# A hybrid attention and pooling block on one core: the query tiles' cosine products on VectorE, and one token sum between the two gate halves

## The reference, cut to what matters

```python
z = rms_norm(h, norm_gain)                       # h: 16 meta tokens + 2048 tokens, 1024 wide
proj = einsum("bld,de->ble", z, w_in)
q, k, v, g_attn, u_pool, g_pool = split(proj)
q = partial_rotary(q); k = partial_rotary(k)     # 16 of each head's 64 features turn
o_attn = chunked_window_attention(q, k, v, attn_sinks)
o_pool = multiscale_pool_mixer(u_pool, w_pool, pool_scale)
gated = concat([silu(g_attn) * o_attn, silu(g_pool) * o_pool])
h = h + einsum("ble,ed->bld", gated, w_out)
y = rms_norm(h, final_norm_gain)[:, 16:]
```

## Time and profile before

| what | value |
|---|---|
| time, median of 3 runs | 1256.24 us (1254.01 to 1257.84) |
| the profiled execution's own time | 1256.06 us |
| its span | 1254.3 us |
| PE busy | 1223.2 us, 98% |
| DVE busy | 804.5 us, 64% |
| ACT busy | 583.7 us, 47% |
| POOL busy | 203.6 us, 16% |
| mean granted TensorE clock | 0.994 of full speed |

### The profile page before, as it was taken

The page is one execution under the profiler, slowest core; times in us unless marked ns, Lnnn a source line. Parts: engine busy times, 40 slices in busy tenths (PEclk is TensorE's granted clock), DMA queues, the critical chain, the costliest instruction groups (busy, mean ns, idle before and its releaser), DMA issues.

```text
span 1254.3 us, 16673 instructions
## 1 busy us (share of the span) xinstructions
PE 1223.2 (98%) x6017; PEld 988.2 (79%) x6017; DVE 804.5 (64%) x1280; ACT 583.7 (47%) x1372; POOL 203.6 (16%) x238
## 2 busy tenths in 40 slices
PE   9999988999999999999999999998999999999997
PEld 9788767877777777788888788886777777788886
DVE  6553332366666666876676977666767666696757
ACT  6622221245555555444755334234555555543445
POOL 1157677520000000500001210000000000100000
PEclk9999999999999999999999999999999999999999
DMA  9525665421110101863254313327111101163324
GB/s 356 203 84 185 224 228 196 161 95 34 34 34 34 37 33 49 320 244 117 86 180 170 119 67 101 134 99 262 34 34 37 47 36 35 53 233 101 113 89 168
DMA packets 46319, 152.57 MB, mean 122 GB/s; under 512 B 4656, under 2 KB 8272, under 8 KB 46256
## 3 DMA queue, kind: packets, MB, share of 16 engines
q1 hardware_dynamic: 29328, 90.45, 21.2%
q0 software_dynamic: 16928, 61.25, 13.4%
HBM read 119.70 MB, written 35.91 MB: 124 GB/s over the span
## 4 chain that ended last, share of the span: by engine, by line
PE 83%; DVE 5%; POOL 5%; issue 3%; ACT 2%; DMA 2%; DVEq 0%; SPq 0%; ACTq 0%; POOLq 0%
PE ps L1423 14%; PE ps L1425 14%; PE ps L1424 14%; PE ps L1713 7%; PE ps L1714 7%; PE ps L1715 7%; PE ps L1614 3%; PE ps L1685 2%; PE ps L1659 2%; PE ps L1598 2%; PE ps L1600 2%; PE ps L1599 2%; POOL tq L587 1%; PE ps L1687 1%; POOL ta_g L577 1%
## 5 line engine op out<-in xcount | busy, mean ns | idle before, releaser
L1423 PE MATMUL ps<-zh,wsplit 128*128 128x512 f32 x912 | 362.1, 397 | 11.1 <-DVE gates_all L1089 8.9
L1425 PE MATMUL ps<-zh,wsplit 128*128 128x512 f32 x912 | 357.3, 392 | 0.0
L1424 PE MATMUL ps<-zl,wsplit 128*128 128x512 f32 x912 | 357.1, 392 | 0.0
L987 DVE TENSOR_TENSOR wsplit<-wraw,wsplit 128x1024 fp32r<-128x1024 f32 (+1 forms) x132 | 174.3, 1321 | 113.1 <-ACT wsplit L657 90.9
L1423 PEld LDWEIGHTS ps<-zh,wsplit 128*128 128x128 f32 x912 | 172.5, 189 | 47.2 <-DVE gates_all L1089 10.6
L1425 PEld LDWEIGHTS ps<-zh,wsplit 128*128 128x128 f32 x912 | 172.2, 189 | 37.1
L1424 PEld LDWEIGHTS ps<-zl,wsplit 128*128 128x128 f32 x912 | 172.6, 189 | 34.3
L1713 PE MATMUL ps<-wsplit,gsh 128*128 128x512 f32 x448 | 174.6, 390 | 1.9 <-DVE gsl L1328 1.7
L1714 PE MATMUL ps<-wsplit,gsh 128*128 128x512 f32 x448 | 174.3, 389 | 0.0
L1715 PE MATMUL ps<-wsplit,gsl 128*128 128x512 f32 x440 | 171.2, 389 | 0.0
L657 ACT ACTIVATE wsplit<-wraw 128x1024 fp32r<-128x1024 f32 x112 | 119.7, 1069 | 93.2 <-PE ps L1715 68.2
(11 more groups left out here) (224 smaller groups left out, 1722.0 us busy)
## 6 DMA issues: line engine op xcount, KB each, us to landing
wraw<-wt SPq DMA_DIRECT2D x32, 512.0 KB, 3.2
wraw<-in_wa SPq DMA_DIRECT2D x26, 512.0 KB, 4.2
wraw<-in_wq SPq DMA_DIRECT2D x24, 512.0 KB, 3.5
wraw<-wat SPq DMA_DIRECT2D x17, 512.0 KB, 3.2
tq<-in_wq POOLq DMA_DIRECT2D x8, 1024.0 KB, 6.4
wt<-tq POOLq DMA_DIRECT2D x8, 1024.0 KB, 5.6
wraw<-wc SPq DMA_DIRECT2D x16, 512.0 KB, 3.3
wraw<-in_wb SPq DMA_DIRECT2D x16, 512.0 KB, 3.5
```

The source lines that it names most:

```text
L987: ve.tensor_tensor(wl[:, slot, 0:size], wraw[:, slot, 0:size], wh[:, slot, 0:size].bitcast(F32), ALU.subtract).then_inc(w_lo, 1)
L1423: te.matmul(ps[:, PB[bank], :], w_h, rhs_z(zh, tb, k), start=k == 0, stop=False)
L1424: te.matmul(ps[:, PB[bank], :], w_h, rhs_z(zl, tb, k), start=False, stop=False)
L1425: last = te.matmul(ps[:, PB[bank], :], w_l, rhs_z(zh, tb, k), start=False, stop=k == KT - 1)
```

## The change

It does three things. `times_cos` of the query tiles goes from POOL to DVE, in both halves: a new `times_cos` in DVE's block is called in `pair_a` behind the second `split_lo` and ahead of `rotate`. The key tile's stays on POOL. Sum 2 of half 1's first pair goes from ahead of `swap` to between the two `silu`, ahead of sum 3. The stream's own two lines for the cosines become a call of the new function, with the same instruction at the same place.

```diff
@@ POOL, in for j in range(HT)
                         gp.dma_start(tq[:, :, :], wq[:, j // 2, :, cols].rearrange("q p n -> p q n")).then_inc(t_in, 16)
-                    if h == 0 or j < PAIR0:
-                        times_cos((1 + HT) * h + 1 + j)
                     pair = PAIR0 + j - 1
@@ DVE, behind swap
+                def times_cos(r):
+
+                    dve.wait_ge(rot_sw, r + 1)
+                    ve.tensor_tensor(rotsrc[:, :], rotsrc[:, :], cos_t[:, :], ALU.mult).then_inc(rot_cos, 1)
+
@@ DVE, pair_a
                     swap((1 + HT) * h + 1 + j)
                     split_lo(block_a(h, 4 + 2 * j), 0)
+                    times_cos((1 + HT) * h + 1 + j)
                     rotate((1 + HT) * h + 1 + j, qk[:, :, 1 + j, :])
@@ DVE, half 1
-                    SUMS = [((0, 1, 2), (3,)), ((4, 5, 6), (7,)), ((8, 9), ())]
+                    SUMS = [((0, 1), (2, 3)), ((4, 5, 6), (7,)), ((8, 9), ())]
@@ DVE, half 1, in the stream
-
                             done = r if prod == 3 else r - 1
-                            dve.wait_ge(rot_sw, done + 1)
-                            ve.tensor_tensor(rotsrc[:, :], rotsrc[:, :], cos_t[:, :], ALU.mult).then_inc(rot_cos, 1)
+                            times_cos(done)
                             rotate(done, qk[:, :, done - (1 + HT) * h, :])
```

## The result

Four runs of the changed kernel took 1240.26 us in the median (1239.6 to 1241.6), four of the kernel before 1255.65 (1254.01 to 1257.84). The ratio is 0.9878, with an interval from 0.9859 to 0.9896: faster by 1.2%, outside what run to run can give. The forecast was 1240.6.

What follows compares the result with a forecast made beforehand. PE, busy 98% of the span, bounds the kernel; stalls and lower clock cost 13.03 us in half 0 and 4.05 in half 1. 17.1 - 1.5 = 15.6 us off 1256.24 gives 1240.6 us; range 1238.0 to 1247.5.

Steps and rivals of the forecast that it cites:

- Part 1: Half 0: with the cosines off POOL, whose round outlasts PE's pair, the 13.03 us of stalls go, save a residue.
- S + 6.95: Half 0's pairs: forecast end of the first SiLU without held instructions, in us from the shuffle's start S.
- The residue: Half 0: cost left from POOL's subtractions holding DVE, 1.5 us in all, between bounds of nothing and 7.5.
- S + 10.2: Half 0's pairs: when PE needs the first SiLU, in us from the shuffle's start; 3.2 us to spare.
- one or two: Half 0: DVE instructions forecast as held by POOL's train of four subtractions at 122 to 128.
- three held instructions, just at the limit: Half 0: three holds of some 1.1 us end the SiLU 10.25 us behind the shuffle's start, just at the limit.
- how often?: Half 0: placing POOL's rounds, every 24.9 us from 93, against DVE's pairs; most pairs stay just inside the limit.
- the lock takes much of it back: Rival, half 0: three pairs stall 1.2 us and lose the clock, 9.3 us, giving 1248.3 us; chance 0.14.
- Part 2: Half 1's first pair: sum 2 behind the first SiLU starts the shuffle earlier; no stall, the full 4.05 us won.
- Part 3: The stream's call: the same instruction at the same place, so nothing gained or lost.
- the rival on DVE's side: Rival, half 0: DVE becomes the bound, slower; seven pairs cost 28 us, giving 1267 us; chance 0.02.
- other releaser: Rival: something besides POOL's cosine product holds the SiLU, PE waits as long, 1254 to 1257 us; chance 0.03.

Runs made afterwards that it cites:

- before_no_subs: The kernel before, with POOL's 52 subtractions on weights replaced by memsets of one element: 1244.95 us, ratio 0.9909.
- one_more: The changed kernel, with one more low-part subtraction on DVE in half 0's pairs, a repeat that changes no value: 1254.73 us, ratio 0.9997.
- sums_only: The kernel before, with only the new place of the token sum; the cosine products stay on POOL: 1251.52 us, ratio 0.9971.
- four_more_no_subs: The changed kernel without POOL's subtractions on weights, with half 0's low part written five times instead of once: 1257.12 us, ratio 1.0023.

## Why the prediction held, and where not

**Part 1, the cause.** Right. POOL's lateness came from its round, and `before_no_subs` shows it: a product on POOL costs half 0 no stall once the round is short. The chain without it came out to the hundredth, S + 6.94 where S + 6.95 was forecast, and that was luck in part. From the cosines' product to the addition were 1.45 us and not 1.36, and the addition took 1.14 to its successor and not its full 1.23; the two errors cancel. POOL's last store moved with it, to 247.93, forecast near 247.

**The residue.** Forecast 1.5 us, measured 0.96, but partly by compensation. The meetings were placed by adding up POOL's rounds. The pair that begins at 126.06 had three held instructions, where "one or two" were forecast. The prediction's own rounds, 93 and then every 24.9 us, put a second train at 131.2, beside that pair's addition, and it was not counted. The last three pairs had none, where "one" was said of one of them. The limit was set at S + 10.2 and was S + 9.82. The step behind it takes PE's readiness (S + 10.2) for the limit; the 0.3 us for filling PE again, which the prediction adds to a stall, belongs off it, and gives S + 9.9. So "three held instructions, just at the limit" is a loss of 0.3 to 0.6 us.

**The size of the cost, in its form.** The prediction treated the hits as independent, 1.1 us each, and the expectation of `one_more` followed that rule: at most 1247.5, where 1254.7 was measured. The term that failed in that expectation is the prediction's "how often?": it took POOL's rounds and PE's pairs as given, one beside the other. A stretched pair changes the next meeting, and behind two of the stalls came the clock. The rival "the lock takes much of it back" lay one DVE instruction a pair away, and would then have cost 14.5 us where it was priced at 9.3.

**Part 2.** Right: by the trace the shuffle followed the second sum, PE had no wait for a SiLU in half 1, and the full 4.05 us came back. `sums_only` shows that this part needs nothing of part 1. The second SiLU, behind two sums, ended in time as well.

**Part 3.** Right: nothing.

**The clock.** That 1.66 us did not lower the clock and 2.15 us did was used as a threshold on length: against the lock's rival, and for the point at S + 12.3 of the rival on DVE's side. The runs do not bear it out. Over all thirteen profiled runs, PE's waits for a SiLU in the pairs and for the last rotated tile before scores lowered the clock in none of 9 of 1.1 to 1.7 us, in 1 of 10 of 1.8 to 2.0, in 6 of 13 of 2.1 to 2.3, and in 10 of 12 of 2.7 to 3.3. Among the same waits some ended either way: 1.84 us in `one_more` and in `four_more_no_subs`, 2.29 and 2.28 us in two profiles of the change itself. So length raises the chance and does not settle it. In the change no such stall was left in the pairs, so the forecast did not suffer; the scores' wait and its clock were there before the change too.

**The other rivals.** No other releaser stood behind L528, and DVE did not become the bound, in a kernel as it is. With four more writes a pair it did, by the chain that was drawn for that rival: 2.15 us a pair at the upper clock.

## What to carry to other kernels

A product on a slow helper engine can be harmless or can cost 12 us, and its duration doesn't tell which: compare the helper's round with the period of the work that waits for it, and look at what is queued ahead. When two engines hold each other up and each runs in a loop, compute their periods; a margin smaller than one or two held instructions can turn into a loss in nearly every iteration, so test it by adding one instruction. And where a sum and a product feed the same wait, do each alone, since their gains don't add.

## What the runs showed of the hardware

- DVE's instructions with two SBUF inputs of 128x1024 (1.22 us) and POOL's subtractions of 128x512 (four in 5.4 us) alternated as whole instructions: 2.3 us each on DVE, 8.0 us for four on POOL. The shuffle (1.32 to 1.37) and the SiLU, which reads PSUM (0.67 to 0.69), were never held. The Trainium skill (SBUF — State Buffer, Who interferes with whom) says that the ports which the two engines share are an exclusive lock, and that a VectorE instruction with at most one SBUF input, outside its 2-port modes, is left alone. The rows agree on both; that two loops can be caught in step by it, with 14.4 us lost here, I had not expected.
- Beside POOL's product of 128x1024 (3.36 us) one DVE instruction was held for all of it, 3.42 us, in the kernel before, in `sums_only` and in `before_no_subs`. Where DVE stood waiting, in the kernel before from 132.00 on, the same product took 2.40 us.
- An idle time of PE of 3.10 us, seven times over, lowered the clock to 0.50 in five cases, at 1.6 us each. Of eleven waits of 2.3 us before half 1's scores four lowered it, and of eight of 1.83 to 1.85 us one. A fall can cost more: in `sums_only`, behind a wait of 2.81 us, the pair was 6.0 us too long, 2.9 more than the wait and the 0.3 us for filling PE.
